# Two transformer blocks on one core: weight pieces of 1024 columns, and three steps of the second block in another order

## The reference

```python
def second_block(...):
        hn = rmsnorm_2(x, norm_mix_g[layer])
        proj = hn @ w_in[layer]
        u_pool, m_q, m_k, m_v, m_o, m_i, m_f, a_q, a_k, a_v = jnp.split(proj, offsets, axis=-1)
        y_pool = pool_mixer(u_pool, ...)                    # windowed means
        y_mlstm = mlstm_mixer(m_q, m_k, m_v, m_o, ...)      # conv of q and k, silu, gated scan both ways
        y_attn = attn_mixer(a_q, a_k, a_v, ..., cos, sin)   # head norm, rotary, attention
        x = x + jnp.concatenate([y_pool, y_mlstm, y_attn], axis=-1) @ w_out[layer]
        x = x + mem_cross_attn(rmsnorm_2(x, ...), mem, ...)
        x = x + ec_moe(rmsnorm_2(x, ...), router_w[layer], expert_w_gu[layer], expert_w_down[layer])
    return rmsnorm_2(x, final_norm_g)
```

## Time and profile before

| | |
|---|---|
| median of three runs | 1506.22 us |
| the profiled execution | 1506.21 us |
| its span, first to last instruction | 1503.4 us |
| PE busy, instructions | 1186.3 us, 8858 |
| DVE busy, instructions | 444.5 us, 868 |
| ACT busy, instructions | 378.9 us, 835 |
| POOL busy, instructions | 83.5 us, 92 |
| mean rate of the DMA engines | 335 GB/s |

### The profile page before, as it was taken

The page is one execution under the profiler, slowest core; times in us unless marked ns, Lnnn a source line. Parts: engine busy times, 40 slices in busy tenths (PEclk is TensorE's granted clock), DMA queues, the critical chain, the costliest instruction groups (busy, mean ns, idle before and its releaser), DMA issues.

```text
span 1503.4 us, 20242 instructions
## 1 busy us (share of the span) xinstructions
PE 1186.3 (79%) x8858; PEld 783.2 (52%) x8858; DVE 444.5 (30%) x868; ACT 378.9 (25%) x835; POOL 83.5 (6%) x92
## 2 busy tenths in 40 slices
PE   9999999999997997896756656666566667567676
PEld 8998989999976875442322312222223223123133
DVE  5565776545678854010000000000000000000001
ACT  5655565444554644100000000000000000000001
POOL 0000020000135421000000000000000000000000
PEclk9999999999998999899878888878888778788799
DMA  8435547454553269999999999999999999999996
GB/s 328 151 140 206 186 169 262 183 214 169 210 199 112 102 233 411 408 430 430 431 432 431 431 432 430 431 431 431 429 432 432 432 431 429 431 431 431 428 426 255
DMA packets 34634, 503.88 MB, mean 335 GB/s; under 512 B 4722, under 2 KB 5362, under 8 KB 8819
## 3 DMA queue, kind: packets, MB, share of 16 engines
q1 hardware_dynamic: 30384, 493.17, 78.8%
q10 hardware_dynamic: 4162, 9.43, 1.8%
HBM read 501.54 MB, written 1.05 MB: 334 GB/s over the span
## 4 chain that ended last, share of the span: by engine, by line
issue 62%; PE 30%; DVE 4%; ACT 2%; POOL 1%; DMA 0%; POOLq 0%; ACTq 0%; DVEq 0%
PE PB L99 29%; PE PB L102 1%; DVE SPL L108 1%; POOL SPL L108 1%; ACT SPH L105 1%; DVE CO L116 0%; DVE AQK L108 0%; POOL SM L136 0%; POOL SP L112 0%; DVE XN L116 0%; DVE SM L128 0%; DVE BC L125 0%; DMA GROW<-in_mix_pre_g_dram 0%; DVE MS L131 0%; ACT SP L105 0%
## 5 line engine op out<-in xcount | busy, mean ns | idle before, releaser
L99 PE MATMUL PB<-RING,XS 128*32 128x512 f32 x2048 | 316.2, 765 | 172.2 <-DMA RING<-in_wgu_dram 168.4
L99 PEld LDWEIGHTS PB<-RING,XS 128*32 128x32 f32 x2048 | 71.0, 133 | 367.1 <-DMA RING<-in_wgu_dram 198.3
L99 PE MATMUL PB<-RING,HHT 128*32 128x256 f32 x2048 | 160.8, 474 | 88.7 <-DMA RING<-in_wdn_dram 87.1
L108 DVE TENSOR_TENSOR SPL<-RAW,SPH 128x512 fp32r<-128x512 f32 x306 | 202.8, 721 | 38.5 <-ACT SPH L105 36.3
L99 PE MATMUL PB<-XTH,SPL 128*128 128x256 f32 x704 | 201.7, 287 | 0.0
L99 PE MATMUL PB<-XTH,SPH 128*128 128x256 f32 x704 | 199.2, 283 | 0.0
L99 PE MATMUL PB<-XTL,SPH 128*128 128x256 f32 x704 | 199.1, 283 | 0.0
L105 ACT ACTIVATE SPH<-RAW 128x512 fp32r<-128x512 f32 x340 | 186.6, 621 | 6.5 <-DMA RAW<-in_wst_dram 2.4
L99 PEld LDWEIGHTS PB<-RING,HHT 128*32 128x32 f32 x2048 | 74.0, 133 | 156.7 <-DMA RING<-in_wdn_dram 93.5
L105 ACT ACTIVATE SG<-PB 128x512 f32<-128x512 f32 (+1 forms) x21 | 11.9, 566 | 551.9 <-PE PB L99 549.8
L99 PEld LDWEIGHTS PB<-XTL,SPH 128*128 128x128 f32 x704 | 135.0, 192 | 0.5
(11 more groups left out here) (311 smaller groups left out, 1371.5 us busy)
## 6 DMA issues: line engine op xcount, KB each, us to landing
RING<-in_wgu_dram SPq DMA_DIRECT2D x55, 4096.0 KB, 53.0
RING<-in_wdn_dram SPq DMA_DIRECT2D x28, 4096.0 KB, 52.8
RAW<-in_wst_dram SPq DMA_DIRECT2D x84, 1024.0 KB, 4.9
RING<-in_wgu_dram SPq DMA_DIRECT2D x11, 2048.0 KB, 50.5
RING<-in_wgu_dram SPq DMA_DIRECT2D x14, 1024.0 KB, 6.9
RING<-in_wdn_dram SPq DMA_DIRECT2D x7, 2048.0 KB, 21.2
RAW<-in_wst_dram SPq DMA_DIRECT2D x4, 256.0 KB, 5.1
MEM<-in_mem_dram ACTq DMA_DIRECT2D x1, 1024.0 KB, 7.1
```

The lines of the kernel that those rows point to most:

```text
L99: return pe.do(lambda e: e.matmul(out_, lhsT, rhs, start=start, stop=stop), after)
L108: return on.do(lambda e: e.tensor_tensor(out_, a, b, op), after)
```

## The change

`split_piece` takes a width n of one or two quarters. Two are taken in one ACT and one subtract instruction of 1024 columns, where the subtraction is DVE's, both quarters lie in the same half of the unit, and the unit is not the first one (unit 0, whose quarters are loaded one by one). Both quarters then carry the token of the same instruction. POOL's pieces stay at 512 columns. `bg` and `unit` ask for two where two are left.

In the second block, the second half of the second tile's rotary (`next(rot1)`) moves ahead of the first convolution, between the two `bg(4, 4)`. The turn of the gates becomes a function and moves, with `conv((0, 1))`, behind the first of the two `ua` tiles.

```diff
-    def split_piece(low=dve):
+    def split_piece(low=dve, n=1):
         u, q = divmod(state["piece"], 4)
         if u >= NU or (u >= NSPLIT and u - NSPLIT not in unit_free):
-            return False
-        state["piece"] += 1
-        c = slice(512 * q, 512 * (q + 1))
+            return 0
+        n = n if u and q % 2 == 0 else 1
+        state["piece"] += n
+        c = slice(512 * q, 512 * (q + n))
...
-        parts.setdefault(u, []).append(l)
-        if q == 3:
+        parts.setdefault(u, []).extend([l] * n)
+        if q + n == 4:
             raw_free[u] = (h, *parts[u][::-1])
             stream_load()
-        return True
+        return n
 
     def bg(n, on_pool=0):
 
-        for i in range(n):
-            if not split_piece(pool if i >= n - on_pool else dve):
+        i = 0
+        while i < n:
+            on = pool if i >= n - on_pool else dve
+            done = split_piece(on, 2 if on is dve and n - on_pool - i >= 2 else 1)
+            if not done:
                 return
+            i += done
 
     def unit(u):
         while len(parts.get(u, ())) < 4:
-            assert split_piece(), u
+            assert split_piece(dve, 2), u
...
     conv_product(3)
-    for t in range(2):
-        w = tr(PB[4][:, t * P:(t + 1) * P], MT2[:, t * P:(t + 1) * P], mt, *held[4])
-    pt = PB[4][:, 0:T].rearrange("p (t c) -> p t c", t=2)
-    nac = copy(NAC[:, :, 0:64], pt[:, :, 0:64], w)
-    em = act(NAC[:, :, 64:128], pt[:, :, 64:128], ACT.Exp, nac, scale=-1.0)
-    held[4] = [nac, em]
-    bg(4, 4)
-    conv((0, 1))
     bg(4, 4)
     r1 = next(rot1)
-
+    bg(4, 4)
+
+
+    def turn_gates():
+        for t in range(2):
+            w = tr(PB[4][:, t * P:(t + 1) * P], MT2[:, t * P:(t + 1) * P], mt, *held[4])
+        pt = PB[4][:, 0:T].rearrange("p (t c) -> p t c", t=2)
+        nac = copy(NAC[:, :, 0:64], pt[:, :, 0:64], w)
+        em = act(NAC[:, :, 64:128], pt[:, :, 64:128], ACT.Exp, nac, scale=-1.0)
+        held[4] = [nac, em]
+        return nac, em
 
     up_ok, mv_ok = [], []
     for t in range(2):
@@ -1111,6 +1118,9 @@
         held[6 + t] = [a, m]
         up_ok.append(a)
         mv_ok.append(m)
+        if t == 0:
+            nac, em = turn_gates()
+            conv((0, 1))
     xt_read = w
```

## The result

| | before | after |
|---|---|---|
| median | 1506.69 us (10 runs) | 1511.41 us (10 runs) |
| ratio, 95% interval | | 1.0028, 1.0019 to 1.0037 |
| the profiled execution, its span | 1506.21, 1503.4 us | 1512.11, 1509.3 us |
| DVE busy, instructions | 444.5 us, 868 | 436.0 us, 724 |
| ACT busy, instructions | 378.9 us, 835 | 366.8 us, 691 |

Two executions far above all others, one of the kernel before (2694.5 us) and one of `narrow_4_places` (2135.0 us), are left out of the ratios and spreads.

What follows compares the result with a forecast made beforehand. PE was taken to bound the kernel to about 570 us, then DMA, with DVE and POOL bounding 462 to 486 us. Latencies, savings and the reorder's -1.0 summed to -0.15 us: 1506.0 us, range 1503.2 to 1508.4.

Steps and rivals of the forecast that it cites:

- (b): At 454.09 us, before the scans leading to MT2: DVE waits for a whole wide high part, +0.35 us on its chain.
- a POOL piece costs DVE about 1.0 us whatever DVE step it meets: Reordered stretch: eight POOL pieces meet eight DVE steps before and after, so contention was taken to change by 0.
- (e): Four attention rounds after 487 us, a pair each: savings of -0.3 to one wait of +0.4, taken as +0.15 us.
- (d): At 558.71 us, five pieces ahead of the cross-attention scores' reduction: DVE waits longer for ACT, +0.3 us.
- 146 pairs: Whole kernel: pairs of pieces made wide, so DVE issues 160 splits for 306 and ACT 194 for 340.
- (f): Norm chains between 408 and 432 us: high parts ready long before, four pairs saving 0.07 us each, -0.25 us.
- around 403, 0: Around 403 us PE takes pieces as they come but waits later anyway, so the wide pieces cost 0 there.
- (c): Before 440.13 us, the first rotary: DVE waits for a wide high part, mostly absorbed, +0.15 us (0 to 0.35).
- (a): Unit 1 at 14.15 us: its first wide piece reaches PE later, +0.5 us, never regained (bounds 0 and 0.6).
- one-for-one pass to the end: Expert stage, DMA-bound: it shifts as a block, so any dense-part gain or loss reaches the end in full.
- Rival C: Stretch before the scan scores: ACT's UP and QKT wait behind tanh, three further POOL meetings, 1509.6 us; chance 0.11.
- Rival D: Wide pieces' latencies are hidden everywhere, so only the reorder counts: 1504.9 us; chance 0.17.

Runs made afterwards that it cites:

- narrow_4_places: The changed kernel with units 1, 31, 77 and 83 (and unit 0, as before) kept at narrow pieces; 1.0000 of the kernel before.
- order_only: The kernel before with the new order of the second block alone, pieces still 512 columns; 0.9994 of the kernel before.
- change_again: The whole change run once more, unaltered, on the chip of two other runs and with a second trace; 1.0030 of the kernel before.
- wide_only: The kernel before with the wide pieces alone, in the old order; 1.0043 of the kernel before.

## Why the prediction was wrong

- **The mechanism of the reorder was right.** -1.0 us was forecast, +0.35 of (b) in it, with the wait for MT2 turned into one of 3.1 us for the split (3.19 measured), no wait for AQK, one of 4 to 5 us for UP (3.93), POOL's pieces in one run, and DVE as what bounds it. `order_only` has no (b), so that it should have given -1.35; it gave -0.9. In the changed kernel 0.4 us are seen in one trace (+2.2 to +1.8) and 1.6 in the other (+2.3 to +0.7), with the clock at 0.50 and at 1.00. In the first PE comes last, with DVE ready 0.8 us before it; in the second DVE does. Term (b) was as forecast: DVE's idle time before the scans is 3.89 us for 3.46. PE and DVE of the changed kernel, against the earlier trace rows:

```profile
468.16 0.63 PE L99 MATMUL PB<-SPH,XTL 128*128 128x512 f32 x1 [3.19 <-DVE SPL L108]
483.15 3.68 PE L99 MATMUL PB<-AG,UP 128*64 128x256 f32 x16 [3.93 <-ACT UP L105]
...
456.72 1.23 DVE L108 TENSOR_TENSOR SPL<-RAW,SPH 128x1024 fp32r<-128x1024 f32 x1 [3.89 <-ACT SPH L105]
...
476.60 1.80 DVE L108 TENSOR_TENSOR AQK<-AQK,RT 128x640 f32<-128x640 f32 x1
```

- **The step that failed** is "a POOL piece costs DVE about 1.0 us whatever DVE step it meets", from which, with "eight again" as the count of meetings, the sum took the contention as unchanged. The price for DVE held (1.09 us at 200 us, 1.08 at 565 us), but it is one side only. The other, what a longer DVE step costs POOL's, was not in the sum: +0.9 at 195 us and +0.9 of (e). And the meetings were counted between 457 and 485 us alone, where there were eight again; at 565 us a new one makes 1.1 us of (d).
- **A place was missed.** "146 pairs" counts unit 30 among DVE's; it is POOL's, the saving is 144. The same oversight hid `bg(2, 2)`. Before, PE came to unit 30 after POOL by little, and "PE waits for nothing between 15 and 399 us" says nothing of how little: 1.1 us of longer pieces brought a wait of 0.63 us and a shift of 0.9.
- **(e) was +0.15 and is +2.2** (about as much in four of five traces): 0.9 for the multiplications, the rest for the clock. I had valued the low clock once, behind a gap that was there, and never asked which new gap could bring it.
- **(d) was +0.3 and is +1.4**, as told above. **(f) and "around 403, 0"** were -0.25 and are +0.7 from 216 to 429 us: PE waits for a wide low part at 404.88 (0.43 us) and 428.20 (0.33), and again at 433.11 (0.48), of which shorter waits for XN give part back. The saving of 0.07 us a pair needs a queue of pieces that are all ready; where PE takes them one by one, it waited 0.3 to 0.5 us for the wide one. (c) was +0.15 and is 0.
- **(a), as a wait, and the durations were right** (1.23 and 1.04 us; 1.22 and 1.05 to 1.07 measured), and so, but for its scatter, was the one-for-one pass to the end. The +5.2 at 561.7 us is +5.9 in the span; over all the traces the time behind that landmark is from 1.0 us shorter to 2.5 us longer than in that of before, with a median of 0.8 longer, while the shifts themselves run from -3.7 to +7.6.
- **Two readings were off without touching the sum.** "Up to 22 us" less busy time assumes that a page adds durations up; it counts overlaps once, so the fall of 8.5 and 12.1 us answers to the 10 and 15 us of spacing. And in the list of waits POOL's BD (3.7 us in three waits) stood between AQK and MT2; it is there in both kernels.
- **Rival C was the slower side and priced at 1509.6, but its mechanism,** the wait for UP with further meetings, is not what happened: the loss lies at 14, 195, 404 to 433, 499 and 560 to 566 us. Rival D is refuted: the late pieces were what counted.

## What to carry to other kernels

Making one engine's instructions wider saves its fixed cost only where it is the bound, and is paid wherever another engine takes the first half at once, or shares its port; go through every place where the widened instruction runs beside the other engine, and price both directions. A run of full busy time does not say that its inputs come early: list for each the slack, not the wait. And before work is given to a second engine to relieve the first, compare what its piece takes from the first (1.04 us here) with what the first would need for it (0.61 us).

## What the runs showed of the hardware

- **PE's clock follows its own idle time, but not in every execution alike.** After 3.93 us without work the changed kernel ran at 0.50 (the lower of the two levels, 1.2 GHz) from about 483 to 488 us; in `change_again`, after 2.89 us, it stayed at 1.00 and the 16 matmuls took 1.95 us for 3.68. The shorter wait alone doesn't explain that: in the kernel before 2.82 us without work were followed by matmuls of 0.63 us. The start differs too. The first four matmuls behind the warm-up, before:

```profile
4.16 2.24 PE L99 MATMUL PB<-GROW,WARM 1*128 1x512 f32 x4 [0.17 <-DMA GROW<-in_mix_pre_g_dram]
7.33 1.67 PE L102 MATMUL PB<-CON,XN 128*128 128x128 f32 x8 [0.51 <-DVE XN L116]
```

and in `wide_only`, where no edit has yet run:

```profile
4.30 3.77 PE L99 MATMUL PB<-GROW,WARM 1*128 1x512 f32 x4 [0.31 <-DMA GROW<-in_mix_pre_g_dram]
...
9.00 1.97 PE L102 MATMUL PB<-CON,XN 128*128 128x128 f32 x8 [0.20 <-DVE XN L116]
```

  The same four take 3.77 us instead of 2.24, and the whole trace lies 1.9 us late; the kernel before itself spreads from 1504.5 to 1509.5 us. The granted clock reads 1.00 in both up to 8 us, so it doesn't say why. From 9 to 11 us it reads 0.50 in before's trace and 1.00 in this one, which doesn't fit its rows there: the eight transposes take 1.97 us, where eight at 13.70 us in the changed kernel take 1.32. The Trainium skill, "TensorE: Matmul & The Clock Gate", section "What's actually happening", says that the number of matmuls at the low clock differs from run to run of one kernel at its start; the traces agree, and show the same in mid-kernel.
- **Port contention is paid by both engines.** POOL's piece takes 1.27 us alone, 1.75 with a narrow DVE piece beside it and 2.34 with a wide one, DVE's 1.78 for 0.69 and 2.32 for 1.23. A multiplication of POOL's with one SBUF input (SP) is lengthened as well: 4.18 to 5.10 us for four.
